# One block of programs for projection, attention, mix and feed-forward of a decoder layer

## The reference, cut to what matters

```python
h = _rms_norm(x, norm_mix[l])
proj = h @ w_in[l]                       # q | k | v | B | C | u
attn = _stick_breaking_attention(...)    # 8 heads of 64
conv = _short_conv_mixer(cb, cc, cu, conv_w[l])
x = x + jnp.concatenate([attn, conv], -1) @ w_out[l]
h = _rms_norm(x, norm_ffn[l])
x = x + (jax.nn.silu(h @ w_gate[l]) * (h @ w_up[l])) @ w_down[l]
```

## Time and profile before

| | us |
|---|---|
| runs (3) | 2596.59, 2599.43, 2600.51; median 2599.43 |
| profiled execution | 2598.14, span 2596.4 |
| PE busy in the span | 2463.3 (95%) |
| DVE / ACT / POOL busy | 1414.1 / 1165.6 / 1311.5 |
| mean granted TensorE clock | 0.984 |

### The profile page before, as it was taken

The page is one execution under the profiler, slowest core; times in us unless marked ns, Lnnn a source line. Parts: engine busy times, 40 slices in busy tenths (PEclk is TensorE's granted clock), DMA queues, the critical chain, the costliest instruction groups (busy, mean ns, idle before and its releaser), DMA issues.

```text
span 2596.4 us, 34828 instructions
## 1 busy us (share of the span) xinstructions
PE 2463.3 (95%) x12008; PEld 2032.5 (78%) x12008; DVE 1414.1 (54%) x1463; ACT 1165.6 (45%) x1864; POOL 1311.5 (51%) x916
## 2 busy tenths in 40 slices
PE   8899999999899999799979999999999999999999
PEld 6777877777777777678768888888777888888887
DVE  4333366776676666533665555553645555553343
ACT  3222267676677676432343333324443333332433
POOL 1454366767667677300465445422785544551243
PEclk9999999999999999899989999999999999999999
DMA  5988863443443432254323332348663233224766
GB/s 178 302 264 279 258 182 100 135 107 94 128 107 97 143 90 68 75 173 138 146 89 113 112 119 75 109 170 294 206 205 126 73 109 121 87 99 159 228 216 203
DMA packets 337225, 388.17 MB, mean 150 GB/s; under 512 B 21440, under 2 KB 242752, under 8 KB 334784
## 3 DMA queue, kind: packets, MB, share of 16 engines
q1 hardware_dynamic: 337088, 386.49, 46.9%
HBM read 263.20 MB, written 123.21 MB: 149 GB/s over the span
## 4 chain that ended last, share of the span: by engine, by line
PE 44%; POOL 3%; DMA 1%; DVE 1%; issue 1%; ACT 0%; SPq 0%; DVEq 0%; POOLq 0%; ACTq 0%
PE ffn_ps L2184 10%; PE ffn_ps L2186 10%; PE ffn_ps L2188 10%; PE ffn_ps L2214 4%; PE ffn_ps L2216 4%; PE ffn_ps L2215 4%; POOL ffn_A L2103 1%; DMA ffn_raw<-in_w_up 1%; POOL ffn_A L2108 1%; POOL all_B L2130 0%; DMA ffn_A_over<-in_w_down 0%; ACT ffn_A L1796 0%; DMA ffn_A_over<-x 0%; POOL ffn_s L2114 0%; DVE ffn_A L1975 0%
## 5 line engine op out<-in xcount | busy, mean ns | idle before, releaser
L2103 POOL TENSOR_TENSOR ffn_A<-ffn_raw,ffn_A 128x512 fp32r<-128x512 f32 x264 | 366.1, 1399 | 381.3 <-ACT ffn_A L1754 381.3
L2184 PE MATMUL ffn_ps<-all_B,ffn_A 128*128 128x512 f32 x1232 | 482.1, 391 | 17.8 <-POOL ffn_A L2103 15.3
L2186 PE MATMUL ffn_ps<-all_B,ffn_A 128*128 128x512 f32 x1232 | 481.5, 391 | 0.0
L2188 PE MATMUL ffn_ps<-all_B,ffn_A 128*128 128x512 f32 x1232 | 481.3, 391 | 0.0
L1059 DVE TENSOR_TENSOR_SCAN lay_stick<-lay_ps,lay_stick 128x128 f32<-128x128 f32 (+5 forms) x192 | 331.2, 1726 | 199.5 <-ACT lay_ps L963 189.6
L1110 POOL TENSOR_TENSOR lay_a<-lay_a,lay_stick 128x128 f32<-128x128 f32 (+5 forms) x192 | 281.4, 1472 | 219.9 <-DVE lay_stick L1059 219.1
L1754 ACT ACTIVATE ffn_A<-ffn_raw 128x512 fp32r<-128x512 f32 x264 | 162.2, 626 | 291.0 <-DMA ffn_raw<-in_w_gate 122.8
L2184 PEld LDWEIGHTS ffn_ps<-all_B,ffn_A 128*128 128x128 f32 x1232 | 232.5, 189 | 67.5 <-POOL ffn_A L2103 19.0
L1796 ACT ACTIVATE ffn_A<-ffn_A_over 128x1024 fp32r<-128x1024 f32 x154 | 163.1, 1060 | 253.0 <-PE ffn_ps L2216 227.7
L1975 DVE TENSOR_TENSOR ffn_A<-ffn_A_over,ffn_A 128x1024 fp32r<-128x1024 f32 x104 | 154.5, 1489 | 212.9 <-ACT ffn_A L1796 212.9
L2188 PEld LDWEIGHTS ffn_ps<-all_B,ffn_A 128*128 128x128 f32 x1232 | 232.4, 189 | 48.3
(11 more groups left out here) (135 smaller groups left out, 5036.0 us busy)
## 6 DMA issues: line engine op xcount, KB each, us to landing
hid_ops<-ffn_s SPq DMA_DIRECT2D x154, 256.0 KB, 2.0
ffn_A_over<-hid_ops SPq DMA_DIRECT2D x154, 256.0 KB, 3.0
lay_w_stage<-in_w_in SPq DMA_DIRECT2D x48, 512.0 KB, 4.2
ffn_raw<-in_w_gate SPq DMA_DIRECT2D x22, 1024.0 KB, 5.4
ffn_raw<-in_w_up SPq DMA_DIRECT2D x22, 1024.0 KB, 7.6
ffn_A_over<-wd_ops SPq DMA_DIRECT2D x88, 256.0 KB, 3.5
ffn_A_over<-in_w_down SPq DMA_DIRECT2D x66, 256.0 KB, 3.9
lay_wd_raw<-in_w_down SPq DMA_DIRECT2D x11, 1024.0 KB, 8.5
```

The lines of the kernel that those rows point to most:

```text
L2103: nc.gpsimd.tensor_tensor(A[:, j, p, 1, :, :], operand(j, p), A[:, j, p, 0, :, :].bitcast(F32), ALU.subtract).then_inc(lo_done, 1)
L2184: nc.tensor.matmul(ps[:, b, :], A[:, j, p, 0, k, :], B[p][:, 0, k, :], start=first_mm, stop=False, skip_group_check=True)
L2186: nc.tensor.matmul(ps[:, b, :], A[:, j, p, 0, k, :], B[p][:, 1, k, :], start=False, stop=False, skip_group_check=True)
L2188: mm = nc.tensor.matmul(ps[:, b, :], A[:, j, p, 1, k, :], B[p][:, 0, k, :], start=False, stop=last_mm, skip_group_check=True)
```

## The change

`run` no longer makes a block for each stage. One block holds attention, mix and feed-forward; each engine's list is now attention's list, mix's `main`, and the feed-forward's list. `mix_stage` gives back single operations that the neighbours call:

- Attention's SP list loads w_out pieces 0 and 1 at unit 27 of the last pair and the two first tiles of `mixT` at unit 38, and pieces 2 and 3 before its last two stores. Its POOL list ends with `first_split` of both tiles.
- In attention's leftover units ACT runs both `mix_split` and `w_part(0)` to `w_part(2)`, DVE `w_part(0)` and `w_part(1)`, PE the chunks of w_out pieces 0 and 1 for two tiles.
- Mix's tiles run in the order 6, 7, 4, 5, 2, 3, 0, 1, 8, ..., 15 (`ORDER`); attention's last pair has stored tokens 768 to 1023 by its group 9. Buffers overlay others, with a wait for each (`FREED_BY` in the feed-forward).
- With the third tile, both halves of its matmuls are followed by transposes (tiles at places 0 and 1).
- The tiles at places 14 and 15 are multiplied piece by piece, place 15 three pieces behind place 14 (`STAGGER`); `load_raw(0, ...)` waits for `tail_done` 2.
- The adds, norms, transposes and stores of places 14 and 15 move into the feed-forward's `opening()`; transposes of 14 stand after product 0, those of 15 after product 2.

```diff
+            ops = mix.tensor(pe)
+            att.tensor(pe, ops)
+            ops["main"]()
+            ffn.tensor(pe, ops)
...
             pairs(act, body)
+            for i in range(2):
+                mix["mix_split"](i)
             for n in range(NU - LAG, NU):
                 aT_part(PAIRS - 1, n)
                 if opens[n - 1]:
                     o_part(PAIRS - 1, units[n - 1][0] - 1)
+                mix["w_part"](n - NU + LAG)
...
                 transposes(PAIRS - 1, n)
                 if opens[n]:
                     a_times_v(PAIRS - 1, units[n][0] - 1)
+                if n > NU - LAG:
+                    for i in range(2):
+                        mix["chunk"](i, n - NU + LAG - 1)
             a_times_v(PAIRS - 1, NG - 1)
...
+ORDER = [6, 7, 4, 5, 2, 3, 0, 1] + list(range(8, 16))
...
+        def main():
+            load_w(4)
+            load_w(5)
+            load_mix(2)
             load_x(0)
+            load_w(6)
             load_x(1)
+            load_mix(3)
+            sp.dma_start(gain[:, :], norm_ffn.partition_broadcast(P)).then_inc(gain_in, DMA)
+            load_w(7)
...
+            for k in range(KT + STAGGER):
+                if k < KT:
+                    chunk(TAIL, k)
+                if k >= STAGGER:
+                    chunk(TILES - 1, k - STAGGER)
+                if k == STAGGER:
+                    transposes(TAIL - 1)
...
             def load_raw(R, j):
                 wait(sp, lo_done, NP * (R - 1) + 1 + spot[j, P3])
+                if R == 0:
+                    sp.wait_ge(mix.tail_done, 2)
...
             def opening():
-                for j, p in SUMS[:6]:
+                for j, p in SUMS[:4]:
                     sums(0, j, p)
+                ops["add"](MIXED - 2)
+                for j, p in SUMS[4:6]:
+                    sums(0, j, p)
+                ops["x_norm"](MIXED - 2)
+                ops["add"](MIXED - 1)
+                ops["x_norm"](MIXED - 1)
+                sums(0, GATE, P3)
                 b_lo(0, B21)
...
                 for n in range(NP):
                     product(ROUNDS * G, n, first=True)
+                    if G == 0 and n in (0, 2):
+                        ops["transposes"](MIXED - 2 + n // 2)
```

More of the change, by code:

```diff
@@ L145, with run @@
     tensor: object
-def run(nc, programs):
+def run(nc, att, mix, ffn):
     with nc.Block() as block:
@@ new lines, in whole_layer @@
+        mix["gain"], mix["xn"] = at(s_at + 4 * D, "m_gain", [P, D]), at(s_at + 12 * D, "m_xn", [P, D])
+        m.offset = b_at
+        B, Bf = m.paired("B", 7, [P, 2, KT // 2, BANK])
+        ffn = {"s1": m.at("s1", [P, 2, KT // 2, P]), "s3": m.at("s3", [P, BANK])}
+        mix.update({n: m.at("m_" + n, [P, 1]) for n in ("ss", "msq", "rstd")})
+        ffn["raw"] = at(raw_at, "raw", [P, 2, KT, 2 * P])
+        ffn["A"] = at(slot[0], "A", [P, 2, 7, 2, KT // 2, P], F32R)
+        ffn["Af"] = m.over("A", [P, 2, 7, 2, KT // 2, P], F32)
@@ L814, in pairs, with sync @@
             body(PAIRS - 1)
-        def sync(sp):
+        def sync(sp, mix):
             def load_k(p, h):
@@ L948, in sync @@
             store_y(PAIRS - 1, CT - 1)
-            for gi in range(NG - 3, NG):
+            store_o(PAIRS - 1, NG - 3)
+            mix["load_w"](2)
+            mix["load_w"](3)
+            for gi in range(NG - 2, NG):
                 store_o(PAIRS - 1, gi)
@@ new lines, in tensor, with transposes, chunk, main @@
+    def tensor(pe):
+        def transposes(i):
+            pe.wait_ge(xn_done, i + 1)
+            wait(pe, hT_done, NB * i)
+            for n in range(NB):
+                for j in range(4):
+                    k = 4 * n + j
+                    last = nc.tensor.transpose(tr[:, n, j, :], xn[:, k * P:(k + 1) * P], cst["ident"][:, :])
+                last.then_inc(tr_full, 1)
+        def chunk(i, k):
+            if i < 2:
+                pe.wait_ge(w_lo_done, k + 1)
+            if k == 0:
+                pe.wait_ge(mix_lo_done, i + 1)
+                wait(pe, acc_done, NH * (i - 1))
+            for n in range(NH):
+                cols = slice(n * BANK, (n + 1) * BANK)
+                last = matmul3(nc, ps[:, bank(i, n), :], hi_of(i)[:, k, :], lo_of(i)[:, k, :],
+                               w_hi[k][:, cols], w_lo[k][:, cols], k == 0, k == KT - 1)
+                if k == KT - 1:
+                    last.then_inc(proj_full, 1)
+            if i == TILES - 1 and k < KT - 1:
+                last.then_inc(tail_done, 1)
+        def main():
+            for k in range(WEIGHTS_AHEAD - 1, KT):
+                for i in range(2):
+                    chunk(i, k)
+            for i in range(2, TAIL):
+                pe.wait_ge(mix_lo_done, i + 1)
+                wait(pe, acc_done, NH * (i - 1))
@@ L1744, in hi @@
                 wait(act, prod_done, NP * (R - 1) + n + 1)
+                if R == 0:
+                    place = FREED_BY[n]
+                    if place < 8:
+                        act.wait_ge(mix.tail_done, place)
+                    else:
+                        act.wait_ge(mix.proj_full, NH * (MIXED - 9 + place))
                 if R and R % ROUNDS == 0:
@@ L1759, in keep @@
                 q = (C11, C12, C22)[n]
+                if R == 0 and q == C22:
+                    act.wait_ge(mix.xn_done, MIXED)
                 if j == GATE:
```

593 lines of the change are left out of this document (355 added, 238 removed).

## The result

The changed kernel took 2575.0 us (median of 4; 2570.23 to 2575.99), the kernel before beside it 2598.01 (2596.51 to 2600.51): ratio 0.9907, 95% interval 0.989 to 0.9924. Taken again later it took 2573.7 against 2600.07, ratio 0.9902 (0.9886 to 0.9919). The forecast was 2572, 2561 to 2581.

A forecast was written before the change was run, and what follows sets the result against it. PE was busy 95% of the span, so time could come only from its idle or half-clock stretches, with waits at the two joints. Savings of 8.5 + 18.7 = 27.2 us gave 2572 us, 80% range 2561 to 2581.

The forecast's parts named there:

- The sum: Whole kernel: 8.5 us at attention to mix plus 18.7 at mix to feed-forward, 27.2 us saved.
- First joint, 8.5: Attention to mix: third mix tile starts at 1115.0 instead of 1123.46, 8.5 us earlier; bounds 2.3 and 15.
- Penultimate `a_times_v` +0.7: Attention's leftover units: ACT's two `mix_split` ahead of `aT_part(45)` delay it 0.7 us, to 1075.3 from 1074.63.
- Mix 166.7: Third tile to the last chunk of places 14 and 15: stays at 166.7 us.
- I leave its fall of the clock (1.6) in: Third mix tile: still pays 1.6 us for half clock, since PE has idled 1.9 us just before.
- Second joint, 18.7: Mix to feed-forward: last mix chunk to end of round 0 takes 45.3 us instead of 64.0; bounds 10 and 22.5.
- The 1.1 added to `x_norm`: Norm of place 14 on DVE: `x_norm` takes 1.1 us longer because POOL starts a `lo` alongside.
- The price of the 3.96 us wait: Round 0's product 11, waiting for ACT's `keep(0, UP, 2)`: 3.96 us and a clock fall of 2.4 us disappear.
- After round 0 nothing changes, since the later rounds wait for nothing: Feed-forward rounds after round 0: no change in time, as PE was busy 386.70 of 386.70 us there.
- The third: Rival at both joints, chance 0.14: clock stays up over short gaps, DVE free at once; 15 + 20 us gained, 2563.
- The rule of the Trainium skill: Attention to mix: short bursts between DMA waits run at half clock, pieces 2 to 7; third tile at 1123.
- slower: Rival, chance 0.04: half clock carries on into mix; 27.2 us eaten after 136 matmuls, 2686 if through places 2 to 13.

The follow-up runs named there:

- `keep` early: Kernel before, with ACT's copy `keep(0, UP, 2)` moved ahead of the rounding that waits for raw weights: 2600.37 us, ratio 1.0.
- piece 7 early: Changed kernel, with the load of mix weight piece 7 issued directly behind piece 6 on the SP queue: 2571.29 us, ratio 0.9889.
- small edits: Changed kernel plus unit 47's transposes, piece 7's load, tile 0's add and round 2's raw loads earlier, transposes of places 14 and 15 one product later: 2560.48 us.

## Why the prediction was right

- **The sum.** Forecast 27.2 us up to the start of round 1, measured 27.1 in the profile; the medians gave 23.0 and 26.4 for the whole kernel, and 2575.0 and 2573.7 against the forecast 2572. The mechanism held: undoing either joint costs about its part, 9.5 and 17.8. But the near equality in the profile is partly luck. The joints gave 1.0 and 0.7 less than forecast, and mix 1.6 that had been put at nothing. And attention's tail was 1.76 us late in this profile: counted from unit 45's transposes (1071.28 before, 1073.04) the gain up to round 1 is 28.9 us, in the second profile 29.2. Why the medians show less is not known.
- **First joint, 8.5.** Measured 7.5 from the start of the span, and 9.2 from unit 45's transposes, which in this execution came 1.76 later (1073.04); in the other profile with the old joints, that with `keep` early, they came 2.87 later (1074.15). The clock made up for it: the penultimate `a_times_v` took 3.8 us at full clock (1076.43 to 1080.20), where I had 5.8 from the half clock of before. The forecast waits were 2.5, 2.3, 2.0, 0.9 and about 1.4 at pieces 1, 2, 4, 6 and 7; measured 2.46, 2.05, none, 0.26 and 3.65. The first two steps held, and the last store and piece 4's load behind them came 1.5 us earlier than forecast (1092.25, forecast 1093.8). At piece 4 PE did not wait, because piece 2 ran at half clock: it lasted 4.45 us (1091.32 to 1095.77), piece 3 at full clock 2.74, and so filled time that I had as idle. The term with a wrong size is the transfer: the five loads from piece 6 to piece 7 took 10.3 us (1098.48 to 1108.77), not 7.8. They began 1.4 us earlier than forecast, so "piece 7 lands at 1107.7, ready at 1110.3" came out near, as 1108.8 and 1111.1. PE was through piece 6 at 1107.4 instead of 1108.9, hence 3.65 us of wait instead of 1.4.
- **Penultimate `a_times_v` +0.7.** It started at 1076.43, 3.39 after unit 45's transposes; before, 3.35 (1074.63 - 1071.28). Unit 46's transposes waited 1.72 us instead of 0.65, behind ACT's two splits (1.99 together), but both they and unit 45's ran at full clock (unit 45's took 1.16 us instead of 1.94), which gave it back. So the term was 0, not 0.7.
- **Mix 166.7, "I leave its fall of the clock (1.6) in".** Measured 165.1 in all ten profiles in which the feed-forward follows mix without a wait. The fall came at piece 7 instead, before the third tile, and is in the first joint's number.
- **Second joint, 18.7.** Measured 64.0 - 46.0 = 18.0. The raw weights were issued 12.1 us before T1 (forecast 12.3) and the second was taken at T1 - 3.6 (forecast T1 - 4); product 0 had no gap. Transposes of place 14: idle 3.06 instead of 3.6 and one fall of the clock; no wait at product 11. The norm's step is in these rows of DVE and POOL:

```profile
1284.74 2.28 DVE L1622 SCALAR_TENSOR_TENSOR lay_m_xn<-lay_B_over,lay_m_rstd,lay_m_gain 128x1024 f32<-128x1024 f32 x1 [2.05 <-POOL lay_m_rstd L1509]
1286.95 1.27 DVE L1616 TENSOR_TENSOR lay_B_over<-lay_B_over,lay_ps 128x512 f32<-128x512 f32 x2
```

```profile
1284.68 1.27 POOL L2339 TENSOR_TENSOR lay_A<-lay_s,lay_A 128x512 fp32r<-128x512 f32 x1
1285.90 3.49 POOL L2339 TENSOR_TENSOR lay_A<-lay_raw,lay_A 128x512 fp32r<-128x512 f32 x2
```

- The 1.1 added to `x_norm` was 1.0: 2.28 against 1.285 alone. The Trainium skill ("SBUF — State Buffer", "Who interferes with whom") says that a VectorE instruction with two SBUF inputs contends with a GpSimd instruction that reads SBUF, over a pair of ports that is locked, not shared out. The rows agree: the two adds beside the same POOL work, one of whose inputs is PSUM, took 1.27 together, as fast as alone.
- **The price of the 3.96 us wait** had a wrong size too. Its releaser was right, but taken alone it is worth nothing, since a chain on DVE is as late, 10.5 us on. In the sum this did no harm, because the whole opening moved earlier.
- **"After round 0 nothing changes, since the later rounds wait for nothing"** was nearly wrong. Round 1's product 6 had 0.36 us of wait, and one queued load there was the next bound.
- **The rivals.** None held as a whole. The third had the clock up over short gaps, which was so up to piece 1 (1.00 in the windows of 1070.00 to 1081.00 and 1085.50 to 1089.00). The rule of the Trainium skill ("TensorE: Matmul & The Clock Gate", the section on HAM oscillation), by which the first joint's gain would be near zero, was partly seen: of the bursts behind 2.46, 2.05 and 3.65 us idle the first ran at full clock, while the others fell for part of their stretches. Only pieces 2 and 7 fell, not all of pieces 2 to 7. The clock was back before the third tile, so slower was far off.

## What to carry to other kernels

Where two stages are overlapped, follow each wait back through the in-order queues. Its end is often a load that was issued late behind something that nobody is waiting for: a store of sums, the gain, a tile of x needed later. A wait removed alone may be given back at the next chain, so a set of small edits (together 2575 to 2560 here) is tried as one, after each has shown which wait takes its place. Measure a joint as a distance between two marks on PE, not by the span.

## What had not been expected of the hardware

- The same idle gaps gave different clocks in different executions of the same work. In 1070 to 1081 us the granted clock was 1.00, in the changed kernel's second profile 0.84 over the same work (1072 to 1083), and the kernel before had 0.51 with similar bursts. The burst behind 2.46 us idle ran at 1.00, the stretch behind 2.05 us at 0.87. With piece 7 early it was the other way round: 0.72 in 1085 to 1091, around the burst behind 2.46 us, while the stretch from 1091 to 1116 us stayed at 1.00 with waits of 2.05, 1.24, 0.47 and 2.42. The distance from T1 to round 1 is 46.0 or 44.3 for one kernel mostly by this: the wait at place 14 was 3.06 and 2.79, the clock behind it 0.50 (1287.0 to 1292.5) and 0.75 (1290 to 1296). What decides it stays open.
- A piece of 512 KB took 3.86 us from issue to landing as the first of a group of loads, and 8.34 as the last of five.
- PE's wait without a releaser near 700 us, where attention's loop starts over, was 4.7 to 6.9 us in the executions profiled, and shifts all that follows.
